# An expert-mixture inference step on one core: four of the eight gate/up products in split precision, one down buffer, and logits in four column groups

## The reference

```
logits = einsum('btd,de->bte', h, w_router)            # 16 experts
...                                                    # two experts per token, chosen by sigmoid scores
gate = einsum('btd,edf->btef', h, w_eg)                # 1024 x 256 per expert
up = einsum('btd,edf->btef', h, w_eu)
a = silu(gate) * up * combine
return einsum('btef,efd->btd', a, w_ed)                # 256 x 1024 per expert
```

## Time and profile before

| | us |
|---|---|
| three runs | 1172.09, 1178.92, 1180.94 |
| median | 1178.92 |
| profiled execution, whole | 1171.3 |
| its span | 1169.5 |
| PE busy in the span | 1035.0 (88%) |
| DVE busy | 663.1 (57%) |
| ACT busy | 416.9 (36%) |

### The profile page before, as it was taken

One profiled execution on the slowest core, in us unless ns is written; L12 is line 12 of the kernel. 1 busy time (PEld: TensorE's weight loads), 2 busy tenths in 40 slices (PEclk: granted clock), 3 DMA queues, 4 the chain that ended last, 5 costly groups with the idle time before them and its releaser, 6 DMA issues.

```text
span 1169.5 us, 18117 instructions
## 1 busy us (share of the span) xinstructions
PE 1035.0 (88%) x5952; PEld 790.5 (68%) x5953; DVE 663.1 (57%) x1129; ACT 416.9 (36%) x810; POOL 198.9 (17%) x244
## 2 busy tenths in 40 slices
PE   6899999999999989899878999981699999889950
PEld 3799999999999875578864555551466666556630
DVE  2543885176889311159974343358567666466744
ACT  3443223243322244256650111020444444244513
POOL 2010000000000020013371000000124443224324
PEclk8799999999999999999999999985799999989985
DMA  9643333314433232131145222226557988986839
GB/s 364 255 152 133 118 143 126 109 58 141 143 128 110 73 122 80 45 109 55 55 101 214 108 101 78 91 103 251 185 180 219 300 288 275 287 269 196 229 55 359
DMA packets 58644, 187.38 MB, mean 160 GB/s; under 512 B 7874, under 2 KB 20658, under 8 KB 52450
## 3 DMA queue, kind: packets, MB, share of 16 engines
q1 hardware_dynamic: 46820, 144.92, 34.6%
q0 software_dynamic: 7920, 28.84, 10.6%
q10 hardware_dynamic: 3856, 13.00, 2.9%
HBM read 151.53 MB, written 35.21 MB: 160 GB/s over the span
## 4 chain that ended last, share of the span: by engine, by line
PE 78%; DVE 9%; DMA 5%; issue 3%; ACT 2%; POOL 1%; SPq 1%; ACTq 1%; DVEq 0%; POOLq 0%
PE psum L1279 41%; PE psum L1221 28%; PE psum L1499 2%; DVE RW L1805 2%; DMA RA<-in_w_ada 1%; PE psum L1144 1%; DVE RE L1832 1%; DMA acc_scratch<-RE,idxsc 1%; DMA RB<-in_w_exp 1%; DMA out<-RB 1%; PE psum L1434 1%; DVE RE L1840 1%; PE psum L1236 1%; DMA RW<-gm_scratch 1%; PE psum L1153 1%
## 5 line engine op out<-in xcount | busy, mean ns | idle before, releaser
L1221 PE MATMUL psum<-input_parts,weight_parts 128*128 128x320 f32 x2208 | 339.3, 312 | 1.2 <-DVE input_parts L1604 1.1
L1221 PEld LDWEIGHTS psum<-input_parts,weight_parts 128*128 128x128 f32 x2208 | 325.8, 189 | 10.1 <-issue 6.9
L1279 PE MATMUL psum<-RB,RW 128*128 x324 | 146.9, 604 | 1.6 <-issue 1.5
L865 ACT ACTIVATE weight_parts<-RW 128x1024 fp32r<-128x1024 f32 x46 | 48.7, 1058 | 224.7 <-PE psum L1221 223.6
L1279 PE MATMUL psum<-expert_parts 128*128 128x512 f32 x486 | 126.5, 413 | 1.9 <-DVE expert_parts L2069 1.9
L1611 DVE TENSOR_TENSOR weight_parts<-RW,weight_parts 128x1024 fp32r<-128x1024 f32 x46 | 56.3, 1225 | 113.4 <-ACT weight_parts L865 113.3
L1279 PEld LDWEIGHTS psum<-expert_parts 128*128 128x128 f32 x486 | 91.3, 188 | 32.5 <-issue 14.3
L1279 PEld LDWEIGHTS psum<-RB,RW 128*128 128x128 f32 x324 | 60.7, 194 | 69.2 <-issue 69.2
L1279 PE MATMUL psum<-RS,RB 128*128 128x512 f32 (+1 forms) x200 | 79.9, 553 | 2.0 <-DVE RE L1832 1.2
L1279 PE MATMUL psum<-RC,RB 128*128 128x512 f32 x160 | 71.5, 600 | 0.0
L679 POOL TENSOR_TENSOR RE<-RE,RA 2x2304 f32<-2x2304 f32 (+1 forms) x2 | 9.0, 4516 | 358.4 <-DMA RA<-in_b_ada 358.3
(11 more groups left out here) (334 smaller groups left out, 1477.9 us busy)
## 6 DMA issues: line engine op xcount, KB each, us to landing
RB<-in_w_exp SPq DMA_DIRECT2D x48, 1024.0 KB
RW<-in_w_in SPq DMA_DIRECT2D x46, 512.0 KB, 4.2
RW<-in_w_ada SPq DMA_DIRECT2D x34, 512.0 KB, 3.4
RA<-in_w_ada SPq DMA_DIRECT2D x10, 512.0 KB, 15.5
RW<-gm_scratch SPq DMA_DIRECT2D x20, 256.0 KB, 3.4
h_scratch<-RE SPq DMA_DIRECT2D x10, 512.0 KB, 2.6
acc_scratch<-RA SPq DMA_DIRECT2D x10, 512.0 KB, 3.6
RB<-acc_scratch ACTq DMA_DIRECT2D x10, 512.0 KB, 7.9
```

Of the source, the lines that this page charges most:

```text
L865: nc.scalar.activation(spl[:, r, 0], raw[:, r], ACT.Copy).then_inc(whi_ok, 1)
L1221: last = nc.tensor.matmul(psum[:, 2 * r + g, 0:GW], spl[:, r, wv, k], hT[:, xv, k, g * GW:(g + 1) * GW], start=(k == 0 and wv == 0 and xv ...
L1279: return nc.tensor.matmul(out, lhsT, rhs, start=start, stop=stop, **kw_)
```

## The change

Four things change. SK becomes 4: four of eight gate/up slices are made from parts, so that a block has 4 whole products (8 records) and 24 single-pass ones; gate_high and gate_low each become two instructions of 1024 columns, and x_chan and x_low handle 512 columns each. The down parts lose their second buffer: `gsplit` holds two blocks of gate/up parts, `dsplit` one block of down parts, which is filled at the beginning of the block's own period, once down(n-1) is done. The order in a period changes with it, on ACT and DVE. And the logits are made another way: `part_logits` puts the router's columns (padded to 32) in as weights of four column groups and streams 128 tokens; ACT copies the four partial sums, and one more product with a matrix of ones and zeros (`gsum4`) adds them. Some small tables move into the unused masks.

```diff
-SK = 2
+SK = 4
...
-        esplit = expert_parts[:, 0:12 * D].rearrange("p (b v n) -> p b v n", b=2, v=2)
+        gsplit = expert_parts[:, 0:8 * D].rearrange("p (b v n) -> p b v n", b=2, v=2)
+        dsplit = expert_parts[:, 8 * D:12 * D].rearrange("p (v n) -> p v n", v=2)
...
+            if t >= 2:
+                logits_part(t - 2)
+            if t == NT - 1:
+                logits_part(t - 1)
             if t == NT - 2:
                 act.wait_ge(lg_ps, BATCH)
...
                 a_high(j, i * 2 + (1 + j))
+                down_high(bass.ds(i * 2 + j, 1), i * 2 + (1 + j))
                 x_chan(j, i * 2 + (3 + j))
+                gate_silu(r, i * 2 + (2 + j))
                 gate_high(j, bass.ds(i * 2 + (2 + j), 1), i * 2 + (1 + j))
-                down_high(r, bass.ds(i * 2 + (1 + j), 1), i * 2 + (1 + j))
-                gate_silu(r, i * 2 + (2 + j))
...
+        def part_logits(t):
+            pe.wait_ge(h2T_ok, t + 1)
+            if t == BATCH:
+                pe.wait_ge(mix_ok, NH * NT)
+            for k in range(KD):
+                g = 32 * (k % 4)
+                last = mm(psum[g:g + 32, 6 if t < BATCH else 7, 256:256 + P], wr[:, k], h2T[t % 2][:, k], k < 4, k >= 4)
+            last.then_inc(lpart_ps, 1)
...
         def logits(t):
-            pe.wait_ge(h2T_ok, t + 1)
-            for k in range(KD):
-                last = mm(psum[:, 6 if t < BATCH else 7, t * NE:(t + 1) * NE], h2T[t % 2][:, k], wr[:, k], k == 0, k == KD - 1)
-            last.then_inc(lg_ps, 1)
+            pe.wait_ge(lpart_ok, t + 1)
+            mm(psum[:, 6 if t < BATCH else 7, t * NE:(t + 1) * NE], part[t % 2][:, :], gsum4[:, :]).then_inc(lg_ps, 1)
...
             if t >= 1:
                 route(t - 1)
+            if t >= 3:
+                logits(t - 3)
             if t >= 2:
-                logits(t - 2)
+                part_logits(t - 2)
+        logits(NT - 3)
+        part_logits(NT - 2)
+        logits(NT - 2)
         route(NT - 1)
-        logits(NT - 2)
+        part_logits(NT - 1)
         logits(NT - 1)
...
         x_trans(0, 16, None)
+        gate_up(0, slice(0, 1), 1, SPLIT0 + 2)
         x_trans(1, 16, 1)
-        gate_up(0, slice(0, 1), 1, SPLIT0 + 1)
...
+        def expert_block(j, n, blk, split):
+            a_low(j, n + 1)
+            gate_low(1 - j, blk(1), 1, split + 4)
+            down_low(blk(0), split + 5)
+            x_low(j, n + 3)
+            gate_mix(n, blk(0))
+            product(1 - j, n + 2)
+            gate_low(j, blk(2), 0, split + 7)
+            out_rows(j, n, blk(0))
```

More of the change, by code:

```diff
@@ L774, in h2_transposed, with logits_part @@
                 .then_inc(h2T_ok, 1)
+        def logits_part(t):
+            act.wait_ge(lpart_ps, t + 1)
+            nc.scalar.activation(part[t % 2][:, :], psum[:, 6 if t < BATCH else 7, 256:256 + P], ACT.Copy).then_inc(lpart_ok, 1)
         def final_square(t):
@@ L1093, in gate_high, with down_high @@
             act.wait_ge(x1_out, 16 * NT)
-            nc.scalar.activation(esplit[:, r, 0, 0:G_U], wexp[:, bass.ds(off, G_U)], ACT.Copy).then_inc(whi_ok, 1)
-        def down_high(r, blk, read):
+            for q in range(2):
+                nc.scalar.activation(gsplit[:, r, 0, q * D:(q + 1) * D], wexp[:, bass.ds(off + q * D, D)], ACT.Copy).then_inc(whi_ok, 1)
+        def down_high(blk, read):
             need = act.value_load(eidI[0:1, blk], min_val=16 * WPART, max_val=16 * WPART * NE)
@@ L1099, in down_high @@
             act.wait_ge(w_full, need)
-            if read is not None:
-                act.wait_ge(dn_ps, read)
+            act.wait_ge(dn_ps, read)
             act.wait_ge(x1_out, 16 * NT)
             for j in range(2):
-                nc.scalar.activation(esplit[:, r, 0, G_U + j * D:G_U + (j + 1) * D], wexp[:, bass.ds(off + (D_U + j * D), D)], ACT.Copy)\
+                nc.scalar.activation(dsplit[:, 0, j * D:(j + 1) * D], wexp[:, bass.ds(off + (D_U + j * D), D)], ACT.Copy)\
                     .then_inc(whi_ok, 1)
@@ L1112, in _ @@
         x_chan(0, 1)
+        gate_silu(0, 1)
+        x_chan(1, 2)
         gate_high(1, slice(1, 2), None)
-        x_chan(1, 2)
-        down_high(0, slice(0, 1), None)
-        gate_silu(0, 1)
         with act.Fori(0, pairs) as i:
@@ L1170, in mod_columns @@
             for m in ADA_ORDER[4 * i:4 * i + 4]:
-                last = nc.tensor.matmul(psum[:, bank, 2 * m:2 * m + 2], row1[:, m * P:(m + 1) * P], gsel[:, :], start=True, stop=True)
+                last = nc.tensor.matmul(psum[:, bank, 2 * m:2 * m + 2], row1[:, m * P:(m + 1) * P], gsel, start=True, stop=True)
             last.then_inc(cols_ps, 1)
@@ L1235, in ada_slot @@
                     pe.wait_ge(ada_ev, rows)
[L1236 removed]
+                    nc.tensor.matmul(psum[0:2, 7 - j, P:2 * P], gsel, part[1 - j][:, :], start=True, stop=True).then_inc(asum_ps, 1)
                 ada(lambda q: psum[q:q + 2, 6 + j, 0:P], 2 + j)
@@ L1275, in _ @@
         pe.wait_ge(part_ok, NADA - ADA_FIRST)
-        nc.tensor.matmul(psum[0:2, 7, P:2 * P], gsel[:, :], part[1][:, :], start=True, stop=True).then_inc(asum_ps, 1)
+        nc.tensor.matmul(psum[0:2, 7, P:2 * P], gsel, part[1][:, :], start=True, stop=True).then_inc(asum_ps, 1)
         def mm(out, lhsT, rhs, start=True, stop=True, **kw_):
@@ L2099, in out_rows @@
                                            gmix.rearrange("p (b c) -> p b c", b=2), ALU.mult, ALU.mult).then_inc(yb_ok, 1)
[L2101 removed]
+        def expert_block(j, n, blk, split):
[7 more added lines that the diff above has]
+            out_rows(j, n, blk(0))
+        gate_low(0, slice(0, 1), 0, SPLIT0 + 1)
+        gate_low(0, slice(0, 1), 1, SPLIT0 + 2)
         x_low(0, 1)
[L2103 removed]
+        product(0, 1)
         x_low(1, 2)
[L2105 to L2106 removed]
+        gate_low(1, slice(1, 2), 0, SPLIT0 + 3)
         for j in range(2):
[L2108 to L2113 removed]
+            expert_block(j, j, lambda d: slice(j + d, j + d + 1), SPLIT0 + 4 * j)
         with dve.Fori(0, pairs) as i:
             for j in range(2):
[L2116 to L2123 removed]
+                expert_block(j, i * 2 + (2 + j), lambda d: bass.ds(i * 2 + (2 + j + d), 1), i * 8 + (SPLIT0 + 8 + 4 * j))
+        last = pairs * 2 + 2
+        a_low(0, last + 1)
+        down_low(bass.ds(last, 1), pairs * 8 + (SPLIT0 + 13))
+        gate_mix(last, bass.ds(last, 1))
+        out_rows(0, last, bass.ds(last, 1))
         for t in range(NT):
```

78 lines of the change are left out of this document (34 added, 44 removed).

## The result

The changed kernel takes 1173.04 us (median of 21 runs, 1164.64 to 1179.99), the kernel before 1179.22 us (21 runs, 1172.09 to 1185.61): ratio 0.995, 95% interval 0.993 to 0.997. It is 6 us faster; 1156, with a range of 1146 to 1171, was forecast. The profiled execution took 1166.35 us with a span of 1164.6, against 1171.3 and 1169.5.

The account below looks back on a forecast made before the run. The prediction took PE (TensorE) to bound the kernel. Terms -8.6, -8.6, -2.3, +1.2 and -1.6 sum to -19.9: 1151.4 from 1171.3, 1155.9 from the runs' mean, 1159.0 from the timed median; forecast 1156, range 1146 to 1171.

Parts of the forecast that it names:

- the second term, the stops: Expert stage, out(0) to out(25): of 11.5 us of stops 2.9 stay, at expert 11; -8.6 us, bounds -11.5 and -4.
- periods: Expert stage: two more slices in parts save PE 0.34 us a block, period 10.37 to 10.03; -8.6 us over 25 periods.
- first block (turn): Start of the expert stage: whole products start earlier and are four, not six; -2.3 us, bounds 0 and -4.
- last block: Block 26: down parts are made only after a_high(26), so PE waits and may run at half clock; +1.2 us.
- logits (tiles): Tile stage: partial logits save PE time, mostly lost to the first sigmoid moving behind tile 9's projection; net -1.6 us.
- adds set the pace, mildly: Rival, expert stage: adds of rows take 10.8 us each and outrun their buffer, 6 us lost, 1162; chance 0.12.
- The slow-adds rival: Expert stage: POOL's copies and issue stretch beside busy DVE, an add and the period take 11.6 us, 1193; chance 0.06.
- DVE as the bound: Rival, expert stage: 15% more per DVE instruction makes the period 10.45 us, 11 us lost, 1167; chance 0.08.
- Column groups: Rival, logits: column groups don't overlap, sixteen records take 1.75 us, the logits term becomes +8.5, 1166; chance 0.10.
- parts bring nothing: Rival, expert stage: added passes take 0.28 us instead of 0.229, so 8.6 us of gain go, 1165; chance 0.04.

Follow-up runs that it names:

- the runs without loads: Weights of experts 3 to 15 left out: in the kernel before, ratio 0.988; in the changed kernel, 1.001; in the changed kernel with plain writes for adds, 0.978.
- the run with early reads: Changed kernel with register reads put ahead of waits the engines have anyway, second readings of the landed count dropped: ratio 0.9896, block stage 261.9 us.
- without reads: Changed kernel with experts 3 to 15 not loaded and no register reads of the weights' place in the expert stage: ratio 0.990, block stage 252.4 us.
- without the addition: Changed kernel with weights of experts 3 to 15 left out and adds replaced by indirect writes that don't add: ratio 0.980, block stage 252.2 us.
- gathers first: Changed kernel with POOL issuing the gather of block n+5 ahead of the add of block n: ratio 0.9918, block stage 265.9 us.

## Why the prediction was wrong, point by point

The failed step is the second term, the stops: of 11.5 us 2.9 were to stay, and 13.7 us were measured. All terms, from the stages:

| term | forecast | profiles |
|---|---|---|
| periods | -8.6 | -6.9 |
| stops | -8.6 | +2.0 |
| first block (turn) | -2.3 | -2.2 |
| last block | +1.2 | +2.1 |
| logits (tiles) | -1.6 | -0.4 |
| sum | -19.9 | -5.4 |

(The spans differ by 4.9; the rest lies ahead of these stages and behind them.)

**Periods: right in kind, a little less in size.** Blocks without stops take 259.1 in the old kind and 252.2 in the new (the runs without loads, the second with plain adds). The period is 10.09 and not 10.03, and the old one 10.36 on average, not 10.37. "All deadlines hold with 1.3 us to spare or more" was right for durations, and so was that the single down buffer costs nothing inside the loop.

**Stops: wrong, in two ways.** I let 2.9 of 11.5 us stay, all at expert 11, and put every other stop at nothing. Expert 11 cost 10.35 us in the kernel before (periods 16 and 17) and costs 3.96 in the changed one, a gain of 6.4 where 8.6 was forecast; the others went from 1.4 us to 9.7. First, expert 11: I took its landing at 12.1 us from one row; the copy that waits for it started 13.2 us after the issue in the changed kernel, and 13.0 to 16.2 in the nine others that load it. PE reached the place 11.2 us after down(15) in the run with early reads, as the forecast's 11.4 had it; there the stop is 8.7 us, 6.6 of wait and the rest low parts and products at a lower clock. Second, the layout of the period had each engine's instructions and "0.2 for register reads", but not where these reads fall. In the old order, in period 20 of the kernel before, ScalarE's copies end 1.7 us ahead of silu and its reads stand at +1.4 to +3.4, ahead of the stretch behind the add, whose issue ends at +4.3; none of ScalarE's reads was slow. In the new one two reads stand between silu and the gate copy, on the path to the low parts that PE waits for, and an add at +2.95 stretches both. That it does, and what it costs, is shown by the runs without loads, without reads and without the addition, and by the one with reads early.

**The rival "adds set the pace, mildly"** was nearest. Adds did fall behind (issued up to 7.0 us after their rows began, by 5.7 after their end) and POOL's part did stretch; they did not hold the rows but the gathers behind them in the queue, of which the forecast had said that they "have time": leads fell from 13 or more to 10.5. Two stops of 2.0 us are its share. **The slow-adds rival** had its stretch right: issue of an add 1.66 to 2.22 us on average, its copy 0.31 to 0.75. It did not become 1193, since the mean step of the adds stayed near the period. **DVE as the bound** was wrong: it works 40.9 of 50 us, and with reads out of the way 42.4, at a period of 10.09. **Column groups** overlap: sixteen records of partial products take 0.65 us, beside 1.75 for the rival. (The rule of the Trainium skill cited in the prediction, TensorE: Matmul & The Clock Gate, "The mechanism", would have led to some 3 us, an estimate from the lengths of L1144's records; the trace speaks against it.) And the products of the added slices took the 0.23 us of the others, so "parts bring nothing" was wrong too.

**Logits: the mechanism right, the size small.** The sigmoid moved to 770.13 (768.8 forecast, as the projection itself ended later), x1(9) to 778.59 (777.2), and the tail of 5.2 was 5.20.

**First block and last block.** Seven runs have the same code in the turn: it takes 59.3 in the changed kernel and 60.8 to 61.1 in the six others, beside 61.5 before. So the forecast's 2.3 may be as little as 0.4 to 0.7. The last down product started 6.5 us after down(25)'s end and not 4.9; two reads ahead of the copies in front of it took 0.89 and 1.05 us, and in the four kernels with early reads it starts after 4.4. This term was +2.1, not +1.2.

**The range** took no rival in which the stops grow; the bounds of that term were -11.5 to -4.

## What to carry to other kernels

When a change moves work to a new place in a period, move the register reads, semaphores' owners and queue neighbours with it in the plan: a read that an engine does between two dependent instructions is on the path, and in this kernel its length was set by a transfer that doesn't appear beside it in the rows. Test such a layout with its disturbances taken away one at a time; the run without loads, which was meant to be the easy bound, was the slower one and gave the cause. A gain of the period that isn't seen in the time has gone to whatever was hidden until then: find each stop by period number before the next edit, since, when one goes (gathers first), another can grow (expert 11).

## What was unexpected of the hardware

- In these kernels an indirect transfer that adds to its target stretches other engines' register reads from 0.28 to up to 1.55 us, from about 0.6 to 3.0 us after the end of its issue, on TensorE, VectorE, ScalarE and SyncE alike. The same scatter without the addition doesn't, nor do gathers. What in the addition does it is open.
- Less traffic made the kernel slower (1.001 without loads, beside 0.995 with them), as it fixed the adds at a place where they stretch reads in every period.
- POOL's copy of one column takes 0.18 us alone and up to 1.21 beside VectorE's subtractions, and the issue of an add from 1.6 to 2.55:

```profile
1008.71 1.21 POOL L743 COPY idxsc<-maskb 128x1 uint32 x1 [4.74 <-DVE RE L2127]
1010.09 2.40 POOL L744 DMA_INDIRECT acc_scratch<-RE,idxsc  x1 [0.17 <-issue]
```

All 19 copies of this kind over 0.2 us in the changed kernel end 0.04 us after the end of a VectorE operation with both operands in SBUF, such as these subtractions; six that begin while VectorE's operation has an operand in PSUM take 0.18. The Trainium skill (SBUF — State Buffer, "SBUF: two separate sides") says that a VectorE operation with two inputs in SBUF and a POOL operation that reads SBUF exclude each other; the trace's 19 copies agree. The same section of the Trainium skill says that a transfer and a compute operation cannot slow each other. A register read is not a compute operation, and the 512 slow reads show that it is slowed beside an adding transfer; by which path a register read goes no run here shows.
